# Three low parts of the formed activations made by GpSimd instead of VectorE, in the mix stage of an encoder layer

## The reference, cut to what matters

```python
gates = jax.nn.sigmoid(u @ w_gate + b_gate).reshape(bsz, seq, 3, D_MODEL)
mixed = (gates[:, :, 0] * (ya @ w_proj_a)
         + gates[:, :, 1] * (yb @ w_proj_b)
         + gates[:, :, 2] * (yc @ w_proj_c))
h = h + rmsnorm(mixed @ w_out, g_post_mix)
```

## Time and profile before

| what | value |
|---|---|
| median of three runs | 852.69 us |
| the profiled execution | 852.27 us, of which 850.5 us are the span of its instructions |
| PE busy | 841.6 us |
| DVE, ACT, POOL busy | 68%, 53%, 46% of the span |
| granted TensorE clock | 0.998 of full speed |
| the mix stage's unit 2 on PE | starts at 340.33 us of the span |
| pitch of units 4 to 6 | 18.26 us |

### The profile page before, as it was taken

One profiled execution on the slowest core, in us unless ns is written; L12 is line 12 of the kernel. 1 busy time (PEld: TensorE's weight loads), 2 busy tenths in 40 slices (PEclk: granted clock), 3 DMA queues, 4 the chain that ended last, 5 costly groups with the idle time before them and its releaser, 6 DMA issues.

```text
span 850.5 us, 13030 instructions
## 1 busy us (share of the span) xinstructions
PE 841.6 (99%) x4388; PEld 719.4 (85%) x4388; DVE 581.5 (68%) x1146; ACT 446.9 (53%) x826; POOL 390.3 (46%) x524
## 2 busy tenths in 40 slices
PE   9999999999999999999999999999999999999997
PEld 7888888888888888899998899888888888888885
DVE  6677787788766668865544466555555555799895
ACT  6566666877666654444452445443333444455562
POOL 5554434243333446986677326555555555000002
PEclk9999999999999999999999999999999999999999
DMA  8541223322222222344337533333333333245484
GB/s 235 147 125 51 79 72 95 95 76 81 82 81 81 63 62 67 107 120 116 87 103 249 168 124 103 120 109 109 109 113 116 117 117 117 81 162 195 154 279 163
DMA packets 137624, 100.66 MB, mean 118 GB/s; under 512 B 7431, under 2 KB 122063, under 8 KB 137572
## 3 DMA queue, kind: packets, MB, share of 16 engines
q1 hardware_dynamic: 136666, 96.81, 37.0%
q10 hardware_dynamic: 906, 3.20, 1.1%
HBM read 91.81 MB, written 8.17 MB: 118 GB/s over the span
## 4 chain that ended last, share of the span: by engine, by line
PE 93%; DVE 3%; POOL 1%; ACT 1%; issue 0%; DMA 0%; DVEq 0%; SPq 0%; POOLq 0%
PE banks L1975 26%; PE banks L1977 26%; PE banks L1976 26%; PE banks L2151 2%; PE banks L2060 2%; PE banks L2059 2%; PE banks L2390 1%; PE banks L2388 1%; PE banks L2389 1%; PE banks L2123 1%; PE banks L2130 1%; POOL ring_lo L865 1%; PE banks L2114 1%; PE banks L2252 1%; PE banks L2251 1%; PE banks L2250 1%
## 5 line engine op out<-in xcount | busy, mean ns | idle before, releaser
L781 POOL TENSOR_TENSOR ring_lo<-ring_raw,ring_hi 128x256 fp32r<-128x256 f32 x412 | 317.2, 802 | 290.2 <-ACT ring_hi L919 290.0
L1975 PE MATMUL banks<-u_hi,ring_hi 128*128 128x512 f32 (+1 forms) x720 | 277.1, 385 | 0.1
L1977 PE MATMUL banks<-u_hi,ring_lo 128*128 128x512 f32 (+1 forms) x720 | 272.3, 378 | 0.0
L1976 PE MATMUL banks<-u_lo,ring_hi 128*128 128x512 f32 (+1 forms) x720 | 271.9, 378 | 0.0
L1977 PEld LDWEIGHTS banks<-u_hi,ring_lo 128*128 128x128 f32 x720 | 135.4, 188 | 25.7
L1975 PEld LDWEIGHTS banks<-u_hi,ring_hi 128*128 128x128 f32 x720 | 135.6, 188 | 23.8 <-DVE u_lo L1375 0.3
L1976 PEld LDWEIGHTS banks<-u_lo,ring_hi 128*128 128x128 f32 x720 | 135.7, 189 | 23.3
L1814 DVE SCALAR_TENSOR_TENSOR wide<-banks,cols,wide 128x511 f32<-128x511 f32 x88 | 65.9, 749 | 96.9 <-ACT wide L1260 91.4
L919 ACT CAST ring_hi<-ring_raw 128x1024 fp32r<-128x1024 f32 x104 | 108.2, 1042 | 29.3 <-PE banks L1977 24.8
L1260 ACT ACTIVATE wide<-banks,cols 128x512 f32<-128x512 f32 x44 | 34.2, 778 | 98.0 <-PE banks L1977 98.0
L788 POOL TENSOR_SCALAR norm_ms<-norm_ss 128x1 f32<-128x1 f32 x15 | 5.7, 379 | 138.2 <-ACT pages L929 138.1
(11 more groups left out here) (277 smaller groups left out, 1568.1 us busy)
## 6 DMA issues: line engine op xcount, KB each, us to landing
ring_raw<-in_w_ffn_up_dram SPq DMA_DIRECT2D x88, 256.0 KB, 3.2
ring_raw<-in_w_in_dram SPq DMA_DIRECT2D x60, 256.0 KB, 3.4
ring_raw<-in_w_ffn_down_dram SPq DMA_DIRECT2D x55, 256.0 KB, 3.1
ring_raw<-in_w_gate_dram SPq DMA_DIRECT2D x48, 256.0 KB, 3.2
ring_raw<-in_w_out_dram SPq DMA_DIRECT2D x16, 256.0 KB, 3.0
second_tokens<-wide SPq DMA_DIRECT2D x10, 384.0 KB, 3.8
scratch<-second_tokens SPq DMA_DIRECT2D x10, 384.0 KB, 4.0
scratch<-in_x_dram SPq DMA_DIRECT2D x4, 512.0 KB, 4.8
```

The costliest lines, as they stand in the source:

```text
L781: last = pool.tensor_tensor(wlo[:, r, c], raw[:, r, c], whi[:, r, c].bitcast(F32), ALU.subtract)
L1975: pe.matmul(out, lhs_hi, rhs_hi, start=start, stop=False)
L1976: pe.matmul(out, lhs_hi, rhs_lo, start=False, stop=False)
L1977: return pe.matmul(out, lhs_lo, rhs_hi, start=False, stop=stop)
```

## The change

The low parts of u forms 1, 3 and 2 of the second half (three DVE instructions of 128x512, line 1638) are taken from DVE's queue. POOL makes them in six passes of 128x256, behind the low part of tile (2,0) and ahead of the weight forms of unit 2, and counts them in a semaphore of their own, `u_late_lo`. Who waited for `u_form_lo` 6 or 8 waits for 3 or 5 of it and for `u_late_lo` 3.

```diff
+        u_late_lo = sem("u_late_lo")
...
+            def u_forms_low():
+                pool.wait_ge(u_form_hi, 6)
+                for q in (1, 3, 2):
+                    hi, lo = u_form(q, slice(2, 4))
+                    for k in range(2):
+                        last = pool.tensor_tensor(lo[:, k, :], u_raw(U_RAW[q], 1)[:, k, :], hi[:, k, :].bitcast(F32),
+                                                  ALU.subtract)
+                    last.then_inc(u_late_lo, 1)
...
                     n = m - PLAIN
+                    if n == 0:
+                        u_forms_low()
                     form_low(n, 2, 4 * n + 1)
                     form_low(n, 1, 4 * n + 2)
                     quarter_low(mix_tile(m, 1), 1, 1)
...
                     act.wait_ge(mix_lo, m - 1)
-                    act.wait_ge(u_form_lo, 8)
+                    act.wait_ge(u_form_lo, 5)
+                    act.wait_ge(u_late_lo, 3)
...
             u_forms(1)
-            u_forms_low(1, (1, 3, 2), 6)
             weight_sums(PLAIN)
             weight_sums_rest(PLAIN)
             u_forms_low(0, (4,), 7)
...
                 if n == 0:
-                    pe.wait_ge(u_form_lo, 6)
+                    pe.wait_ge(u_form_lo, 3)
+                    pe.wait_ge(u_late_lo, 3)
                 pe.wait_ge(w12_lo, 2 * n + 1)
...
                 if n == 0:
-                    pe.wait_ge(u_form_lo, 8)
+                    pe.wait_ge(u_form_lo, 5)
                 pe.wait_ge(w_lo_done, mix_tile(m, 1) + 1)
```

## The result

The changed kernel takes 853.62 us (median of 22 runs, 853.36 to 854.5) against 852.73 us before (22 runs, 852.16 to 853.37). The ratio is 1.0013, with a 95% interval of 1.0007 to 1.0018: slower by about 0.9 us. The interval lies above 1, so the sign is clear, and the size is under the 0.2% that the prediction took as the least a measurement of this kernel tells. The profiled execution has a span of 852.0 us (before: 850.5). Of these 1.5 us some 0.4 lie ahead of unit 2, which began at 340.75 instead of 340.33; among the ten traces of this study that start lies anywhere from 340.22 to 341.33 whatever the edit.

The account below looks back on a forecast made before the run. PE was taken to bound the kernel, its unit 2 stalls hanging on POOL's end of (2,1): 1.7 us later, less the 0.64 slack, gives + 1.1 on 852.69, so 853.8, written as 853.6, range 852.3 to 855.0 us.

Parts of the forecast that it names:

- What binds: Unit 2's chain: POOL's end of (2,1) sets line 1711 and branch product 0, with 0.64 us of slack from line 1686.
- its head start: DVE before unit 2: line 1652 can be issued 3.5 us sooner, which alone brings nothing.
- POOL's pace: POOL's twelve passes up to (2,1): eight met, 12.0 us, ending at 346.15 instead of 344.46, 1.7 us later.
- The price of a meeting: A POOL pass beside a DVE SBUF-to-SBUF instruction costs 0.45 us more than its 0.70 us alone.
- The stall at the forms: PE in unit 2: a new wait of 0.8 to 1.0 us at form 2, perhaps 0.1 to 0.3 at form 1.
- the limit of 2.2 us: If stalls at forms 2 and 1 together pass 2.2 us, they and not line 1711 set branch product 0.
- The old stall: PE's wait of 1.15 us at branch product 0 in unit 2, claimed to cover the new stall at the forms.
- From (2,1) to line 1711: (3,1) lands 1.7 us later, line 1652 starts 1.1 later, then 2.71 us as before; branch product 0 + 1.1 us.
- Paid once: From unit 3 on, everything shifts as a whole without new PE waits, so the + 1.1 us is paid only once.
- The stalls did not go away: Rival for unit 2: POOL unhindered, (2,1) at 342.55, both old stalls fall away, 851.2 us; chance 0.08.
- Nothing to see: Rival: (2,1) is only about 0.8 us late and the 0.64 us slack eats it, 852.8 us; chance 0.20.
- The clearly slower case: Rival: POOL waits 0.60 us per meeting, (2,1) 2.9 us late, 854.9 us; all twelve met at 0.45, 855.6; chance 0.15.

Follow-up runs that it names:

- e2: Changed kernel with POOL's ten passes put ahead of the quarter of (2,1), in the order PE wants them, PE waiting for each by itself: 853.61 us.
- e1: Kernel before with only DVE's order changed: unit 2's four weight sums ahead of the three late u low parts: 851.73 us, ratio 0.9989.
- e3: Changed kernel with POOL's six new passes cut to three one-column instructions, leaving DVE's relief alone: 850.93 us, ratio 0.9981.
- e5: Changed kernel with four DVE instructions that POOL's passes meet made one column wide, POOL's work unchanged: 852.10 us, ratio 0.9995.
- e7: Kernel before with unit 2's weight sums ahead of the late u low parts and line 1686 moved behind line 1720: 851.00 us, ratio 0.9981.
- e8: Kernel before with line 1686 alone moved behind line 1720: 852.19 us, ratio 0.9994.

## Why the prediction was right

The sum gave 853.8 us, slower by 1.1 us, and 853.6 was written for it; measured are 853.62 and + 0.9. That the two numbers agree to 0.02 us is luck, since terms that were off by 0.2 to 0.5 us, up and down, stand behind it. By its steps:

- **What binds.** That the time hangs on POOL's end of (2,1), and not on the stalls at the forms, is shown by e2 (stalls at the forms removed, nothing gained) and by e1 and e3, in which (2,1) comes sooner and so does branch product 0. But the prediction also says that DVE ahead of unit 2 is not what is late, and that its head start alone brings nothing. That was wrong: in e3 DVE's relief alone brought 1.6 us, because POOL's passes on the weight forms began at u - 4.0 instead of u - 2.2. The sum was not hurt, since in it POOL is busy with the new passes.
- **POOL's pace.** Twelve passes were put at 12.0 us, eight of them met. They took 12.2 us, from 334.60 to 346.81, and eight were met: six of the new ones and two of the next four. The price of a meeting, 0.45 us, is shown by e5. Against the unit's start (2,1) was 1.9 us late, forecast 1.7.
- **The stall at the forms** was mis-sized: forecast 0.8 to 1.0 us at form 2, measured 1.52, since one of the two passes of weight form 2 met line 1691 (the former 1678) and took 1.24 us. I had let both run beside DVE's reads of PSUM. With 1.9 us lost at the forms in all it stayed 0.27 us short of setting branch product 0, nearer to the limit of 2.2 us that I had named than I thought. The old stall did serve as cover.
- **From (2,1) to line 1711** the terms were off and nearly cancelled. POOL was 0.2 us later than forecast, and the load took 3.33 instead of 3.07 us from its second issue, so line 1652 began 1.57 and not 1.1 us later against the unit's start. But it then took 0.69 instead of 1.23 us, where I had kept the old 2.71 us to the end of line 1711. It did meet a pass; it began 0.05 us ahead of it, and the pass was the one stretched. Together + 1.04 us at the end of line 1711; forecast + 1.1. That these offset each other is luck: in e2 the same meeting went the other way, and unit 2 was 0.56 us longer.
- **Paid once.** PE shows no new wait in the units after it; from the start of unit 3 to the end of the span it is 490.2 us before and 490.3 us after.
- **The rivals.** The stalls did not go away, because POOL's hole filled with passes at 1.17 us. "Nothing to see" needed (2,1) to be about 0.8 us late; it was 1.9. The clearly slower case needed a meeting at 0.60 us; in the rows it stays at 0.45 (a pair each 1.15 us). The whole-instruction lock of the Trainium skill, "SBUF — State Buffer", section "SBUF: two separate sides", is right in kind here: SBUF to SBUF instructions of DVE stretched, those that read PSUM (0.67 us beside a pass) did not. In length it is not borne out by a row of meetings, where a pair takes 1.15 us and not the sum of both.

## What to carry to other kernels

Work moved from VectorE to GpSimd is not taken out of the way: where both read two operands from SBUF, a pass and an instruction in a row of meetings each lose time, so count the meetings on both sides and look at what else stands in either queue. A new stall ahead of an old one on the bounding engine costs nothing up to the old one's size; find the later of the two chains before pricing either. And when an idle hole is to be filled, try first to start what already waits behind it sooner: here the same instructions in another order on VectorE gained 0.8 us (the interval just excludes no change), with one more moved 1.6 us, where the transfer lost 0.9.

## What the runs showed of the hardware

- In a row of meetings the stretch is mutual and steady: a 128x256 GpSimd pass and a 128x512 VectorE instruction in alternation start every 1.15 us each, against 0.70 and 0.60 us alone. That is 0.15 us less than one after the other would take by these steps.
- At the first meeting of a row only one of the two was stretched, and starts a few hundredths of a microsecond apart went either way: the VectorE instruction that began at 350.70, 0.05 us ahead of the pass, kept 0.69 us and the pass took 1.24; in e2 the two began at 350.20 and 350.19, and it was 1.28 and 0.74. What decides between them was not tested.
- Three GpSimd subtractions of one column took 1.96 us in e3, against 2.1 us for three of 256 columns alone. DVE ran beside them in steps of 0.60 us, so whether this is a fixed cost of a pass or a wait for DVE is open.
- The load of 256 KB on which the chain hangs took 3.07 us before and 3.33 us after, from its second issue to landing. In the other eight traces it took 3.2 to 3.4 us, also in e1, e7 and e8, which put nothing more on GpSimd. So the longer load is not shown to come from the change; the one trace of the kernel before is the short one, and nothing run here tells why.
